# Adding the last expert's part to the stored output rows by an indirect DMA, in a hybrid attention and mixture-of-experts block on one core

## The reference

```python
x = x + mix @ w_out[l]                       # x2 in the kernel
h2 = rms_norm(x, norm2_g[l])
...
for e in range(N_EXPERTS):                   # 32
    hid = jax.nn.silu(t @ w_gate[e]) * (t @ w_up[e])          # t = h2, 512 x 1024
    y = y + gates[:, e:e + 1] * (hid @ w_down[e])             # gates is 0 but for 2 experts
return x + y
```

## Time and profile before

| | us |
|---|---|
| median of 3 runs | 1084.1 (1084.0 to 1084.58) |
| the profiled execution: its own time | 1084.14 |
| its span in the trace | 1082.4 |
| outside the span | 1.74 |

### The profile page before, as it was taken

The page is one execution under the profiler, slowest core; times in us unless marked ns, Lnnn a source line. Parts: engine busy times, 40 slices in busy tenths (PEclk is TensorE's granted clock), DMA queues, the critical chain, the costliest instruction groups (busy, mean ns, idle before and its releaser), DMA issues.

```text
span 1082.4 us, 13000 instructions
## 1 busy us (share of the span) xinstructions
PE 1056.9 (98%) x5078; PEld 683.3 (63%) x5078; DVE 546.1 (50%) x1030; ACT 343.8 (32%) x620; POOL 290.1 (27%) x197
## 2 busy tenths in 40 slices
PE   7999999999999999999999999999999999999998
PEld 6777888777788888888888863444444444433333
DVE  4533895698850432239994363333333333333334
ACT  6355732454442555541233311111111111111111
POOL 6833344455552444453333010000000000000000
PEclk9999999999999999999999999999999999999999
DMA  8613333224051322244459989999999999999995
GB/s 213 164 40 78 78 78 78 59 78 117 20 129 37 88 69 68 59 145 147 117 194 365 330 343 426 427 425 427 427 426 427 427 426 426 426 428 427 427 427 239
DMA packets 117598, 263.39 MB, mean 243 GB/s; under 512 B 11808, under 2 KB 97824, under 8 KB 104224
## 3 DMA queue, kind: packets, MB, share of 16 engines
q1 hardware_dynamic: 113792, 255.75, 63.1%
q0 software_dynamic: 2352, 4.18, 1.1%
q10 hardware_dynamic: 1392, 2.62, 0.6%
HBM read 262.33 MB, written 4.20 MB: 246 GB/s over the span
## 4 chain that ended last, share of the span: by engine, by line
PE 88%; DMA 10%; DVE 1%; issue 1%; ACT 1%; SPq 0%; POOL 0%; DVEq 0%; ACTq 0%; POOLq 0%
PE bank L656 19%; PE bank L1109 17%; PE bank L675 14%; PE bank L1125 9%; PE bank L911 8%; DMA arena<-w_exp_gu_in 8%; PE bank L1002 4%; PE bank L1131 2%; PE bank L883 2%; PE bank L866 2%; PE bank L1132 2%; PE bank L1096 1%; PE bank L1115 1%; PE bank L874 1%; PE bank L751 1%; PE bank L813 1%
## 5 line engine op out<-in xcount | busy, mean ns | idle before, releaser
L2141 POOL TENSOR_TENSOR piece_r<-arena,piece_r 128x1024 fp32r<-128x1024 f32 x84 | 202.7, 2421 | 240.5 <-ACT piece_r L1270 240.2
L1109 PE MATMUL bank<-arena,work 128*64 128x512 f32 x1024 | 227.1, 593 | 7.4 <-DMA arena<-w_exp_gu_in 7.2
L656 PE MATMUL bank<-piece_r 128*128 128x512 f32 (+1 forms) x936 | 218.6, 389 | 0.0
L656 PEld LDWEIGHTS bank<-piece_r 128*128 128x128 f32 x936 | 172.5, 188 | 35.9 <-issue 3.5
L1109 PEld LDWEIGHTS bank<-arena,work 128*64 128x64 f32 x1024 | 73.5, 137 | 153.6 <-issue 136.2
L1999 DVE TENSOR_TENSOR arena<-bank,arena 128x512 f32<-128x512 f32 x126 | 81.8, 682 | 174.4 <-PE bank L1132 174.0
L675 PE MATMUL bank<-piece_r 128*128 128x512 f32 x672 | 155.8, 391 | 0.5 <-ACT piece_r L1270 0.5
L675 PEld LDWEIGHTS bank<-piece_r 128*128 128x128 f32 x672 | 125.3, 188 | 29.2 <-issue 3.5
L1270 ACT ACTIVATE piece_r<-arena 128x1024 fp32r<-128x1024 f32 x83 | 87.5, 1058 | 98.6 <-DMA arena<-w_branch_gla_in 49.5
L2257 POOL DMA_INDIRECT arena<-x_rows,idx_pair x15 | 15.1, 1010 | 325.8 <-PE bank L1096 310.0
L2017 DVE TENSOR_TENSOR piece_r<-bank,piece_r 64x512 fp32r<-64x512 f32 x64 | 44.1, 689 | 87.5 <-ACT piece_r L1508 86.5
(11 more groups left out here) (278 smaller groups left out, 1123.4 us busy)
## 6 DMA issues: line engine op xcount, KB each, us to landing
arena<-w_exp_gu_in SPq DMA_DIRECT2D x57, 2048.0 KB, 28.0
arena<-w_exp_down_in SPq DMA_DIRECT2D x18, 2048.0 KB, 25.4
arena<-w_in_in SPq DMA_DIRECT2D x68, 512.0 KB, 4.9
wdn_spare<-w_exp_down_in SPq DMA_DIRECT2D x8, 2048.0 KB, 24.8
arena<-w_exp_gu_first_in SPq DMA_DIRECT2D x4, 2048.0 KB, 11.1
arena<-w_exp_gu_in SPq DMA_DIRECT2D x6, 1024.0 KB, 7.9
arena<-w_exp_down_in SPq DMA_DIRECT2D x5, 1024.0 KB, 8.8
wdn_spare<-w_exp_down_in SPq DMA_DIRECT2D x5, 1024.0 KB, 13.1
```

The lines of the kernel that those rows point to most:

```text
L656: last = mm(bank[n % 2][:, cols], w[:, k, :], h[:, k, cols], start=(i == 0 and k == 0), stop=(i == 2 and k == K - 1))
L1109: last = mm(onto[hf * WIDE:(hf + 1) * WIDE, :], hTe[q][:, k, :], both[2 * k // K][:, k % (K // 2), :, hf * HALF:(hf + 1) * HALF], start=(k ...
L2141: Q.tensor_tensor(quarter(w_lo, q), quarter(w_raw, q), quarter(w_hi, q).bitcast(F32), ALU.subtract).then_inc(s["wlo_ready"], 1)
```

## The change

Only expert 30 is combined by matmuls in the last pair. Before that, the token numbers of expert 31's slots in `tok_pair` are overwritten with 512, which matches no token, and kept, turned into row numbers, in `add_rows` (the output seen as 1024 half rows of 512 floats; partitions 64 to 127 hold feature half 0, the others half 1). The order of the end changes: expert 30's down product comes before expert 31's gate and up product, and the last pair's eight tiles come before expert 31's down product, four of them ahead of its transposes. All eight tiles go through VectorE and SP. The four identity matmuls and ScalarE's two copies and stores are gone. Expert 31's down product is copied by ScalarE from PSUM to `last_y`, and GpSimd, behind its branch over the overflow path, waits for all eight stores and for that copy and adds `last_y` to the stored output with an indirect DMA (128 half rows; a row number of 1024 or more is skipped). The overflow path is rewritten the same way. In SP's order D30 moves ahead of loads 62 and 63.

```diff
-            ahead = 3 if q and e < NE - 1 else 4
+            ahead = 3 if q else 4
...
-                if e >= DOWN_AHEAD and e < NE - 2:
+                if e >= DOWN_AHEAD and e < NE - 1:
                     sp.wait_ge(s["y_ready"], e - 2)
                     load_down(e)
...
-            sp.wait_ge(s["y_ready"], NE - 4)
-            load_down(NE - 2)
...
+            for j in range(TILES):
+                hf, t = divmod(j, T)
+                sp.wait_ge(s["x_added"], last_added(j))
+                sp.dma_start(outd[:, t, hf * BLK:(hf + 1) * BLK], x2[:, t, hf * BLK:(hf + 1) * BLK])\
+                    .then_inc(s["out_stored"], 16)
...
+            product(NE - 2)
+            combine(front)
+            transposes_of(NE - 2)
             down_of(NE - 2)
+            front, back = combined_in(NE - 1)
+            combine(front + back)
+            product(NE - 1)
+            pe.wait_ge(s["x_added"], TILES * (PAIRS_E - 1))
+            combine_last(range(T))
+            transposes_of(NE - 1)
+            combine_last(range(T, TILES))
             down_of(NE - 1)
...
+            act.wait_ge(s["y_ready"], NE)
+            A(last_y, bank[1][:, :], ACT.Copy).then_inc(s["last_y"], 1)
...
-            for i, (j, b) in enumerate(COPIED.items()):
...
-                A(x2[:, t, hf * BLK:(hf + 1) * BLK], bank[b][:, :], ACT.Copy).then_inc(s["act_s"], 1)
...
+            V.tensor_scalar(add_rows[WIDE:P, :], odd_rows, 2.0, None, ALU.mult).then_inc(s["add_rows_ready"], 1)
+            V.tensor_scalar(add_rows[0:WIDE, :], odd_swapped, 2.0, 1.0, ALU.mult, ALU.add)\
+                .then_inc(s["add_rows_ready"], 1)
+            dve.wait_ge(s["add_rows_ready"], 2)
+            st.did(V.memset(odd_rows, float(S)))
+            st.did(V.memset(odd_swapped, float(S)))
+            st.settle()
...
+            front, back = combined_in(NE - 1)
+            add_combined(front[:1])
+            low_parts(NE - 2)
+            add_combined(front[1:] + back)
             pick_tokens(PAIRS_E - 1)
+            gated(NE - 1)
+            for j in range(TILES):
+                dve.wait_ge(s["comb_ps"], last_added(j))
+                add_tile(j, bank[LAST_BANKS[j % len(LAST_BANKS)]][:, :]).then_inc(s["x_added"], 1)
...
+            def add_to_rows(rows, y, done):
+                pool.indirect_dma_start(
+                    out=out_half_rows, out_offset=bass.IndirectOffsetOnAxis(ap=rows[:, 0:1], axis=0),
+                    in_=y, in_offset=None, bounds_check=2 * S - 1, oob_is_err=False,
+                    compute_op=ALU.add).then_inc(done, 16)
...
+            pool.wait_ge(s["add_rows_ready"], 2)
+            pool.wait_ge(s["last_y"], 1)
+            pool.wait_ge(s["out_stored"], 16 * TILES)
+            add_to_rows(add_rows, last_y, s["last_rows_added"])
+            pool.wait_ge(s["last_rows_added"], 16)
```

More of the change, by code:

```diff
@@ L258, in encoder_block @@
         pick = [piece_r(11, 512, at) for at in (3584, 1024)]
-        m_pick = [piece_r(0, 512, 512 * hf) for hf in range(2)]
+        last_y, more_y = [piece(0, words=512, off=at) for at in (0, 512)]
         m_scratch = piece(0, words=D, off=1024)
@@ L275, in encoder_block @@
         hid = bias[3][:, 0:256]
[L276 to L280, removed]
+        hidT = bias[3][:, 256:512].rearrange("p (c h s) -> p c h s", c=2, h=2)
         tok_iota = sb("tok_iota", [P, S])[:, :]
@@ L329, in encoder_block @@
         row_more = sb("row_more", [P, 2], I32)
-        tok_more = sb("tok_more", [P, 2])
+        tok_more = sb("tok_more", [P, 1])
+        add_rows, more_rows = [sb(name, [P, 1], I32) for name in ("add_rows", "more_rows")]
         names = """setup_done g1_loaded wsm_loaded small_loaded ms_ready xn_ready xT_ready hT_hi_ready hT_lo_ready
@@ L424, in encoder_block @@
         COMB_BANKS = (2, 3, 6)
-        COPIED = {3: 0, TILES - 1: 4}
-        ADDED = [j for j in range(TILES) if j not in COPIED]
+        LAST_BANKS = (2, 3, 6, 4, 7)
         def last_added(j):
-            return TILES * (PAIRS_E - 1) + ADDED.index(j) + 1
+            return TILES * (PAIRS_E - 1) + j + 1
         DOWN_AHEAD = NE // 2
@@ L1144, in combine, with combine_last @@
                     combine_tile(bank[COMB_BANKS[c % 3]][:, :], pick[hf], y_hi[p % 2][hf], y_lo[p % 2][hf], t, s["comb_ps"])
-            def combine_last():
+            def combine_last(tiles):
                 p = PAIRS_E - 1
[L1149 to L1153, removed]
+                for j in tiles:
                     hf, t = divmod(j, T)
@@ L1156, in combine_last @@
                         pe.wait_ge(s["pick_ready"], 2 * p + hf + 1)
[L1157 to L1164, removed]
+                        pe.wait_ge(s["y_lo_ready"], 4 * p + hf + 1)
+                    if j >= len(LAST_BANKS):
+                        pe.wait_ge(s["x_added"], last_added(j - len(LAST_BANKS)))
+                    combine_tile(bank[LAST_BANKS[j % len(LAST_BANKS)]][:, :], pick[hf], y_hi[p % 2][hf], y_lo[p % 2][hf],
+                                 t, s["comb_ps"])
             def product(e):
@@ L1186, in down_of @@
                     pe.wait_ge(s["y_lo_ready"], 2 * e)
-                down(y_bank(e), [wdn_half(e, h) for h in range(2)], e % 2, s["y_ready"], hidT_of(e),
+                down(y_bank(e), [wdn_half(e, h) for h in range(2)], e % 2, s["y_ready"], hidT,
                      (s["wdn_last"], 16) if e == NE - 1 else None)
@@ L1228, in _ @@
                     pe.wait_ge(s["hidT_ready"], t + (NE + 1))
+                    pe.wait_ge(s["last_y"], t + 1)
                     down(bank[1], [wdn[0][:, h] for h in range(2)], 0, s["y_ready"])
[L1230 to L1238, removed]
         @block.scalar
@@ L1533, in _ @@
                 evict_y(e)
[L1534 to L1538, removed]
+            silu(NE - 2)
+            evict_hidT(NE - 2)
+            evict_y(NE - 2)
+            silu(NE - 1)
+            evict_hidT(NE - 1)
+            act.wait_ge(s["y_ready"], NE)
+            A(last_y, bank[1][:, :], ACT.Copy).then_inc(s["last_y"], 1)
             n_more = act.value_load(own_i[0:1, MORE:MORE + 1], min_val=0, max_val=MORE)
             with act.If(n_more > 0):
[L1542 removed]
+                act.wait_ge(s["comb_ps"], TILES * PAIRS_E)
                 with act.Fori(0, n_more) as t:
@@ L2039, in _ @@
             pick_tokens(0)
+            odd_rows, odd_swapped = [tok_pair[rows, hf, PAIRS_E - 1:PAIRS_E]
+                                     for rows, hf in ((slice(WIDE, P), 0), (slice(0, WIDE), 1))]
+            V.tensor_scalar(add_rows[WIDE:P, :], odd_rows, 2.0, None, ALU.mult).then_inc(s["add_rows_ready"], 1)
[5 more added lines that the diff above has]
+            st.settle()
             for e in range(2, NE - 2):
@@ L2076, in _ @@
                     for hf in range(2):
-                        V.tensor_scalar(m_pick[hf], tok_iota, tok_more[:, hf:hf + 1], None, ALU.is_equal)\
-                            .then_inc(s["m_pick"], 1)
+                        rows = slice(hf * WIDE, (hf + 1) * WIDE)
+                        V.tensor_scalar(more_rows[rows, :], tok_more[rows, :], 2.0, float(hf), ALU.mult, ALU.add)\
+                            .then_inc(s["add_rows_ready"], 1)
                     dve.wait_ge(s["m_rs"], t * 3 + 3)
```

68 lines of the change are left out of this document (20 added, 48 removed).

## The result

| | before | after |
|---|---|---|
| median, us | 1084.14 (1083.76 to 1085.16, 8 runs) | 1087.62 (1087.14 to 1088.75, 8 runs) |
| ratio | 1 | 1.0029, 95% interval 1.002 to 1.0038 |
| the profiled execution | 1084.14 | 1087.93 |
| its span | 1082.4 | 1086.2 |

The changed kernel is slower by 3.5 us. The forecast was 1084.0 with a range to 1087.0, and slower had a chance of 0.22.

What follows compares the result with a forecast made beforehand. Loads bound the kernel to about 1067, TensorE from 1049.04 to its last matmul. Stores landed 1076.9, DMA start 1077.7, X 4.1 to 1081.8, end 0.5 later: span 1082.3, plus 1.74 outside, 1084.0; range 1082.2 to 1087.0.

Steps and rivals of the forecast that it cites:

- What bounds the end: End of kernel: weight loads, then TensorE from 1049.04; ScalarE's copy (1076.75) and the stores (1076.9) nearly tie.
- The loads: Last loads: D30 lands at 1053.9, 62 at 1058.8, 63 at 1063.7, a step of 4.9, each before its use.
- TensorE's path: TensorE's new order at the end: expert 31's down product ends at 1076.1 against 1077.54, 1.4 earlier.
- The stores: Eight stores beside expert 31's down product: last landing about 1076.9, from 1069.9 + 6.8 to 7.2.
- From release to start: GpSimd, from its last condition to the start of the indirect DMA: 0.77, so start at 1077.7.
- X: Last accumulating indirect DMA, start to landing: taken as 4.1, between 2.75 and 8.5; this forecast had chance 0.48.
- the base: Part of the last DMA's time without accumulation: 2.75, a 256 KB store's landing with GpSimd's 1.0 for descriptors.
- the accumulation: Part of the last DMA's time for reading old rows before adding: 1.35, a round trip of 1.2 to 1.4.
- The prediction's other estimate, 2.6: Last DMA by the skill's rule for a GpSimd DMA of 262 KB: 2.6, giving a sum of 1082.5.
- The rival of the dear add: Last DMA with nothing to hide it: 8.5 gives 1088.4, decides from 6.4; slower, chance 0.22.
- The end 0.5 behind, as before: End of kernel: span ends 0.5 after the last DMA's landing at 1081.8, giving 1082.3.
- Small edits at no cost: VectorE's row number operations and memsets near 650 us: covered by a product, otherwise under a microsecond.

Runs made afterwards that it cites:

- h_loads_only: Kernel before, with D30 loaded ahead of loads 62 and 63 and TensorE's old order kept: 1089.45 us, ratio 1.0046.
- b_no_overflow: Changed kernel without the overflow path and its branches on all five engines: 1085.53 us, ratio 1.0014.
- d_plain_write: Changed kernel, but the last indirect DMA overwrites the rows instead of adding to them: 1086.2 us.
- i_before_pool_waits: Kernel before, with GpSimd too waiting for the eight stores at its end, no add: 1085.86 us, ratio 1.0018.
- j_both_act: Changed kernel without the overflow path, and ScalarE instead of GpSimd waits for the last add: 1084.45 us, ratio 1.0003.
- a_sp_waits: Changed kernel, but SyncE instead of GpSimd waits for the last add's landing: 1086.27 us, ratio 1.0019.
- g_both: Changed kernel without the overflow path, and SyncE instead of GpSimd waits for the last add: 1086.03 us, ratio 1.0017.
- m_hoisted: Changed kernel, overflow path kept, TensorE branching ahead of product(31) and ScalarE waiting for the last add: 1085.26 us, ratio 1.0008.

## Why the prediction was wrong, point by point

- **What bounds the end.** Right up to product(31): the loads up to 1049, then TensorE. Behind it the chain of the changed kernel runs over VectorE's adds and the stores, not over TensorE's last down product: ScalarE's copy was done at 1077.5, 2.0 ahead of the last store's landing. The prediction had the two as nearly tied.
- **The loads.** Right, shown by `h_loads_only`: landings moved by one load's 4.9, and nobody waited for them in the new order.
- **TensorE's path.** Right to 0.1: 1076.13 against 1076.1, counted from load 61's landing.
- **The stores.** The step "1069.9 + 6.8 to 7.2 gives about 1076.9 for the last landing" failed. It was 1079.46, or 1078.8 counted from the same release, 1.9 late. Data rate and queueing were as forecast (`b_no_overflow`: 1077.0). What was missing is another user of the DMA engines, the program's own code. The trace of before held it: one q8 packet at 1070.6, 4.5 ahead of the first store, when nothing else was being moved. I read the queue table of the page only for the data queues.
- **From release to start.** 0.96 instead of 0.77: 0.2 too little.
- **X.** 3.5 instead of 4.1, and both bounds held. By `d_plain_write` the base, priced at 2.75, is 2.3, and the accumulation, priced at 1.35, is 1.2, half of it in the issue (1.65 instead of 1.0). The base was priced for 256 KB, but rows that are skipped move nothing: the DMA's queue moved 0.09 MB. The prediction's other estimate, 2.6, was 0.9 too low for the add. The rival of the dear add, which was to carry a slower result, is refuted; the time came out slower by other steps.
- **"The end 0.5 behind, as before".** Failed, and it is the plainest error: 0.5 was read from a kernel in which ScalarE and SyncE were last, and carried to one in which GpSimd is. It is 2.3, of which 1.79 are GpSimd's DRAIN where SyncE's and ScalarE's take 0.01. `i_before_pool_waits` shows 1.8 for that alone.
- **The sum.** 1082.3 forecast for the span, + 0.7 of an earlier start of the traced kernel before, + 1.9 the last store, + 0.2 the start of the DMA, - 0.6 X, + 1.8 the exit is 1086.3; 1086.2 was measured. Two terms that the prediction held fixed gave the loss, and the one that it held open was fine. All the bounds had been put around X.
- **Small edits at no cost.** Not tested alone. Nothing in the traces speaks against it; `j_both_act`, which holds them all, is level with the kernel before.

## What to carry to other kernels

When the last instruction moves to another engine, what follows the last landing moves with it and has to be priced for that engine: here a final wait on GpSimd instead of ScalarE or SyncE cost 1.8 us. Giving it to another engine is one line, but it gave back only 1.35, since GpSimd's DRAIN also ran on behind the indirect DMA that it had issued. Look for that DRAIN among the instructions at the program's last line; page and timeline don't show it. Code is loaded over the same DMA engines as data, so the instruction queues belong in the reading of a tail of stores: a 16 KB block that lands among them cost up to 2.1 us here, and the last one came anywhere from 1065.4 to 1077.0, or not at all, with edits of parts that weren't TensorE's too. A trade that takes a few us off TensorE's tail and adds a dependent DMA behind it has to beat that DMA's whole path, 0.96 + 3.5 and the exit, not its data.

## What the runs showed of the hardware

- Behind the landing that GpSimd waited for last, the span ended 2.2 to 2.3 later in four kernels (the changed one, `b_no_overflow`, `d_plain_write`, `i_before_pool_waits`), of which its DRAIN took 1.71 to 1.79. Where ScalarE or SyncE waited last it was 0.4 to 0.5 for stores, with DRAINs of 0.01. Where they waited for GpSimd's indirect DMA it was 1.1, since GpSimd's DRAIN, begun just ahead of that DMA, took 4.61 to 4.66 (`a_sp_waits`, `g_both`, `j_both_act`, `m_hoisted`). What GpSimd does in its DRAIN the traces don't show.
- A transfer of one 16 KB block of code at the end of the program held one DMA engine for 0.96 to 1.69 us (12.0% to 21.1% of sixteen engines in 0.5 us). Where it fell behind the last issue (five traces), the last store landed 4.4 to 4.8 after its issue, with one engine's share late, against 2.63 to 2.65 without it (three traces); where it fell among the issues (three traces), one store took 1.97 or 1.98 to issue instead of 0.33.
- Behind an idle stretch of 3.72 us TensorE's granted clock was 0.50 until 1064.0, and a product of 32 matmuls took 10.00 us instead of 6.87 (`h_loads_only`).
- An indirect DMA of 128 half rows, most of them skipped (0.09 MB moved), that accumulates in HBM took 1.65 to issue and 3.5 from its start to its landing on idle DMA engines, a plain one of the same form 1.04 and 2.3.
